# One 12 KB-row transfer per expert item in place of an 8 KB-row and a 4 KB-row transfer, in a two-layer decoder trunk

## What is computed

```
def moe_swiglu(x, router, w_gate, w_up, w_down):
    '''Top-2-of-8 expert SwiGLU; each routed token is processed only by its selected experts.'''
...
    def block_ffn(args):
        tok, gate, e = args
        xb = xt[tok]
        h = jax.nn.silu(xb @ w_gate[e]) * (xb @ w_up[e])
        return (h @ w_down[e]) * gate[:, None].astype(x.dtype)
```

## Time and profile before

| | |
|---|---|
| median of 3 runs | 1851.79 us (1851.65 to 1855.87) |
| profiled execution | 1854.4 us |
| its span, first to last instruction | 1852.6 us |
| TensorE busy | 1713.2 us, 92% |
| VectorE busy | 1385.1 us, 75% |
| ScalarE busy | 959.0 us, 52% |
| 16 DMA engines, mean over the span | 228 GB/s, 422.46 MB in 76495 packets |
| mean granted TensorE clock | 0.958 |

### The profile page before, as it was taken

The page is one execution under the profiler, slowest core; times in us unless marked ns, Lnnn a source line. Parts: engine busy times, 40 slices in busy tenths (PEclk is TensorE's granted clock), DMA queues, the critical chain, the costliest instruction groups (busy, mean ns, idle before and its releaser), DMA issues.

```text
span 1852.6 us, 35481 instructions
## 1 busy us (share of the span) xinstructions
PE 1713.2 (92%) x13898; PEld 1533.0 (83%) x13898; DVE 1385.1 (75%) x1978; ACT 959.0 (52%) x1439; POOL 125.4 (7%) x99
## 2 busy tenths in 40 slices
PE   6998787899968898799999999999999999999996
PEld 5788766899954467699999899899898998999996
DVE  5355423888869942588888888888888887988985
ACT  1413211555520012477676676677676675776773
POOL 0005100000026630000000000000000000000000
PEclk8999998999988889899999999999999999999998
DMA  7220003554440050299899799799799898898990
GB/s 291 90 91 3 4 2 115 184 181 173 147 182 1 0 221 21 93 359 357 308 357 360 272 359 349 273 352 343 278 356 340 296 354 329 292 363 311 347 344 23
DMA packets 76495, 422.46 MB, mean 228 GB/s; under 512 B 8625, under 2 KB 8881, under 8 KB 41537
## 3 DMA queue, kind: packets, MB, share of 16 engines
q1 hardware_dynamic: 75744, 418.18, 60.8%
q0 software_dynamic: 608, 2.15, 0.3%
HBM read 419.24 MB, written 1.05 MB: 227 GB/s over the span
## 4 chain that ended last, share of the span: by engine, by line
PE 83%; DVE 11%; issue 4%; ACT 2%; POOL 0%; DMA 0%; DVEq 0%; POOLq 0%; ACTq 0%; SPq 0%
PE PS L1041 33%; PE PS L1057 16%; PE PS L928 10%; PE PS L594 8%; DVE SA L1405 2%; DVE SGS L1413 2%; PE PS L1065 2%; PE PS L915 2%; DVE WLO L1437 1%; PE PS L1049 1%; PE PS L576 1%; PE PS L740 1%; DVE SA L1398 1%; PE PS L757 1%; PE PS L609 1%
## 5 line engine op out<-in xcount | busy, mean ns | idle before, releaser
L1437 DVE TENSOR_TENSOR WLO<-EXA,WHI 128x1024 fp32r<-128x1024 f32 x448 | 530.2, 1221 | 89.0 <-ACT WHI L498 88.5
L1041 PE MATMUL PS<-WHI,XGH 128*128 128x256 f32 x1792 | 514.6, 287 | 20.3 <-issue 14.1
L1041 PE MATMUL PS<-WLO,XGH 128*128 128x256 f32 x1792 | 511.6, 285 | 0.0
L1041 PE MATMUL PS<-WHI,XGL 128*128 128x256 f32 x1792 | 511.4, 285 | 0.0
L498 ACT ACTIVATE WHI<-EXA 128x1024 fp32r<-128x1024 f32 x448 | 450.3, 1060 | 0.0
L1041 PEld LDWEIGHTS PS<-WHI,XGH 128*128 128x128 f32 x1792 | 344.1, 192 | 31.3 <-issue 16.2
L1041 PEld LDWEIGHTS PS<-WLO,XGH 128*128 128x128 f32 x1792 | 344.3, 192 | 8.0
L1041 PEld LDWEIGHTS PS<-WHI,XGL 128*128 128x128 f32 x1792 | 344.4, 192 | 0.0
L1442 DVE TENSOR_TENSOR WLO<-EXB,WHI 128x1024 fp32r<-128x1024 f32 x224 | 272.8, 1218 | 2.4 <-ACT WHI L504 2.4
L504 ACT ACTIVATE WHI<-EXB 128x1024 fp32r<-128x1024 f32 x224 | 236.2, 1055 | 7.9 <-PE PS L1057 7.9
L523 ACT ACTIVATE MSG<-PS 128x128 f32<-128x128 f32 x224 | 62.2, 277 | 301.0 <-PE PS L1041 295.1
(11 more groups left out here) (357 smaller groups left out, 2602.9 us busy)
## 6 DMA issues: line engine op xcount, KB each, us to landing
EXA<-in_wmoe SPq DMA_DIRECT2D x224, 1024.0 KB, 7.5
EXB<-in_wmoe SPq DMA_DIRECT2D x224, 512.0 KB, 5.5
FRA<-in_wffn SPq DMA_DIRECT2D x22, 1024.0 KB, 5.9
RING<-in_wsq SPq DMA_DIRECT2D x16, 1024.0 KB, 4.9
FRB<-in_wffn SPq DMA_DIRECT2D x22, 512.0 KB, 3.8
GLUW<-in_wglu SPq DMA_DIRECT2D x8, 1024.0 KB, 12.6
LORA<-in_lora SPq DMA_DIRECT2D x1, 1536.0 KB, 22.3
LORA<-in_lora SPq DMA_DIRECT2D x1, 1152.0 KB, 19.1
```

Source lines behind the costliest of these rows:

```text
L1041: mm = pe.matmul(PS[:, n % 2, 0:T], x[:, k, :], w[:, n % 2, cols], start=k == 0 and m == 0, stop=k == KC - 1 and m == 2)
L1437: tt(WLO[:, n % 2, cols], EXA[n % NSLOT][:, cols], WHI[:, n % 2, cols].bitcast(F32), ALU.subtract)\
```

## The change

The two arrays of slots become one array `EX` of seven slots of 12 KB, in the same memory; an item's weights come with one transfer, `load_item`, and one semaphore per slot (`m_in0` and so on). The transfer waits for `m_blo` of item n - 7, which comes after that item's `m_alo`. The first five items go out without a wait; items 5 and 6 wait for `glu_used`, where A of item 5 did not.

```
-        EXA = [at(f"EXA{n}", [P, NARROW], F32, o) for n, o in enumerate((r(0), r(8), r(16), r(24), r(32), 0, 8))]
-        EXB = [at(f"EXB{n}", [P, D], F32, o) for n, o in enumerate((r(40), r(44), r(48), r(52), r(56), 16, 20))]
+        EX = [at(f"EX{n}", [P, WIDE], F32, o) for n, o in enumerate((r(0), r(12), r(24), r(36), r(48), 0, 12))]
...
-        def expert_in(part, b, n):
-            return S(f"m{part}_in{n % NSLOT}"), (b * (FM // NSLOT) + n // NSLOT + 1) * 16
+        def expert_in(b, n):
+            return S(f"m_in{n % NSLOT}"), (b * (FM // NSLOT) + n // NSLOT + 1) * 16
...
-            def load_a(b, n, ex):
-                sp.dma_start(EXA[n % NSLOT][:, :], wmoe[ex * FM + n][:, 0:NARROW]).then_inc(expert_in("a", b, n)[0], 16)
-
-            def load_b(b, n, ex):
-                sp.dma_start(EXB[n % NSLOT][:, :], wmoe[ex * FM + n][:, NARROW:WIDE]).then_inc(expert_in("b", b, n)[0], 16)
+            def load_item(b, n, ex):
+                sp.dma_start(EX[n % NSLOT][:, :], wmoe[ex * FM + n]).then_inc(expert_in(b, n)[0], 16)
...
             for n in range(5):
-                load_a(0, n, 0)
-                load_b(0, n, 0)
-            load_a(0, 5, 0)
+                load_item(0, n, 0)
             sp.wait_ge(S("glu_used"), 2)
-            load_b(0, 5, 0)
-            load_a(0, 6, 0)
-            load_b(0, 6, 0)
+            load_item(0, 5, 0)
+            load_item(0, 6, 0)
             for n in range(NSLOT, FM):
-                sp.wait_ge(S("m_alo"), 2 * (n - NSLOT + 1))
-                load_a(0, n, 0)
                 sp.wait_ge(S("m_blo"), n - NSLOT + 1)
-                load_b(0, n, 0)
+                load_item(0, n, 0)
...
                 for n in range(FM):
-                    sp.wait_ge(S("m_alo"), b * (2 * FM) + 2 * (n - NSLOT + 1))
-                    load_a(b, n, ex)
                     sp.wait_ge(S("m_blo"), b * FM + n - NSLOT + 1)
-                    load_b(b, n, ex)
+                    load_item(b, n, ex)
...
-                act.activation(WHI[:, n % 2, cols], EXA[n % NSLOT][:, cols], ACT.Copy).then_inc(S("m_ahi"), 1)
+                act.activation(WHI[:, n % 2, cols], EX[n % NSLOT][:, cols], ACT.Copy).then_inc(S("m_ahi"), 1)
```

More of the change, by code:

```diff
@@ L495, in hi_a @@
                 if h == 0:
-                    act.wait_ge(*expert_in("a", b, n))
+                    act.wait_ge(*expert_in(b, n))
                 cols = slice(h * D, (h + 1) * D)
-                act.activation(WHI[:, n % 2, cols], EXA[n % NSLOT][:, cols], ACT.Copy).then_inc(S("m_ahi"), 1)
+                act.activation(WHI[:, n % 2, cols], EX[n % NSLOT][:, cols], ACT.Copy).then_inc(S("m_ahi"), 1)
             def hi_b(b, n, down_done=True):
-                act.wait_ge(*expert_in("b", b, n))
+                act.wait_ge(*expert_in(b, n))
                 if down_done:
                     act.wait_ge(S("m_used"), b * FM + max(n - 1, 0))
-                act.activation(WHI[:, n % 2, NARROW:WIDE], EXB[n % NSLOT][:, :], ACT.Copy).then_inc(S("m_bhi"), 1)
+                act.activation(WHI[:, n % 2, NARROW:WIDE], EX[n % NSLOT][:, NARROW:WIDE], ACT.Copy).then_inc(S("m_bhi"), 1)
             hi_a(0, 0, 0)
@@ L1436, in lo_a @@
                 cols = slice(h * D, (h + 1) * D)
-                tt(WLO[:, n % 2, cols], EXA[n % NSLOT][:, cols], WHI[:, n % 2, cols].bitcast(F32), ALU.subtract)\
+                tt(WLO[:, n % 2, cols], EX[n % NSLOT][:, cols], WHI[:, n % 2, cols].bitcast(F32), ALU.subtract)\
                     .then_inc(S("m_alo"), 1)
@@ L1441, in lo_b @@
                 dve.wait_ge(S("m_bhi"), b * FM + n + 1)
-                tt(WLO[:, n % 2, NARROW:WIDE], EXB[n % NSLOT][:, :], WHI[:, n % 2, NARROW:WIDE].bitcast(F32), ALU.subtract)\
+                tt(WLO[:, n % 2, NARROW:WIDE], EX[n % NSLOT][:, NARROW:WIDE], WHI[:, n % 2, NARROW:WIDE].bitcast(F32), ALU.subtract)\
                     .then_inc(S("m_blo"), 1)
```

## The result

The changed kernel takes 1866.1 us in the median of five runs, the kernel before 1851.8 us beside it: 1.0067 of its time, 95% interval 1.004 to 1.0093. It is slower, by 14 us between the medians here. In a later session the changed kernel took 1866.7 us, 1.008 of the kernel before (1.0063 to 1.0097). No change was forecast, with a range up to 1857, so the forecast was wrong, and the page shows at once where it was right and where not.

What follows compares the result with a forecast made beforehand. TensorE was taken to bound the kernel, with loads hidden. Four terms of 0 and +0.8 us at the loop's return took the 1851.8 us median to 1852.6, stated as 1852.5 us; range 1847 to 1857 us.

Steps and rivals of the forecast that it cites:

- Rival A: Weight stream inside the blocks falls below 360 GB/s and sets TensorE's pace: +24 us, 1876 us; chance 4 in 100.
- rival C: Weight stream binds now and the merge relieves it: 1823 us, likelier 1837; chance 8 in 100 together with shorter return stalls.
- the lead: Item loads, issue to ScalarE's read: the 8 KB part starts one item later, tightest lead 16.2 us, cost 0.
- The landing: Time for an item's single 1.573 MB transfer to arrive: 7 us taken, at most 9.8, covered by the lead.
- the step on the loop's return: Starts of loop rounds 2 to 6: instruction packets wait behind longer weight rows, +0.8 us, bounds -3.1 and +5.0.
- Rival B: TensorE's stalls at the loop's return grow and keep the clock low: 1861.9 us; chance 5 in 100 to pass 1857.4.
- the +3.4 us for the clock: Part of the +5.0 bound: lower clock lasting as long at the two better returns as at the three worse, 2 x 1.7.

Runs made afterwards that it cites:

- the small part first: Kernel before, with both parts of an item issued together behind the `m_blo` wait, 4 KB rows before 8 KB rows: 1855.9 us, 1.0015.

## Why the prediction was wrong

**Right: TensorE bounds the blocks, and the loads are hidden.** 4.37 us per item at the full clock and 217 waits for slots. Rival A (too slow a stream) and rival C (the merge relieves the stream) are both refuted: no wait for a load appeared, and the blocks ran no faster.

**Right: the lead.** It fell by an item and cost nothing, as the small part first shows. The landing was mis-sized: 7 us, at most 9.8, were forecast, 8.5 and 10.6 measured. The tightest lead, item 8 issued at 784.96 and read at 801.16 us, is 16.2 us and covers it.

**Wrong: the step on the loop's return.** It was priced at +0.8 us with +5.0 as the bound. It is +9.0 us in the profiles of the first session and +10.0 in those of the second, by the stalls alone. The step took one row of weights for the unit that the fetch waits behind, 0.47 us of 12 KB in place of 0.31, and argued that since the bytes in flight are the same, nothing more could come. It also counted two packets per return, of which one stands between branch and restart. Both arguments were wrong: the row's length has no part in it (rows of 4 KB in one transfer: 27.4 us), and equal bytes are not equal waits, since the order and the size of the transfers decide how many of them stand ahead. The sum by the rows that the packets show: before, eight rows of 4 KB stood ahead of the fetch on its engine, 8 x 0.16 = 1.3 us, now 6.6 of 12 KB in the mean, 6.6 x 0.47 = 3.1 us. The estimate of 1.8 us per return fits the 1.8 and 2.0 us measured in the two pairs of profiles.

The rows for this were there: the two instruction packets stood in the earlier trace rows, the stalls in the earlier trace rows, and B of an item issued just ahead of A of the next, 0.37 us apart, in the earlier trace rows. What was not asked is what SyncE has in flight when TensorE jumps.

The page "DMA: Bandwidth & Descriptors" of the Trainium skill, section "Queues, rings and completion order", was cited for the +0.8 us, and misread. It says that an engine drains a whole packet, typically 9 to 17 descriptors and at most 64, from one queue before it takes another, while what this profile counts as a packet is one row. A transfer over 128 partitions gives each of 16 engines 8 rows and a semaphore write, 9 descriptors. By that rule the fetch waits out the share of the transfer that stands first. The trace agrees where that is 512 or 1024 KB in two-transfer form: 20 returns of 20 in four profiles. It does not agree at 1536 KB, where the packet went one or two rows before the end of eight, and four or five before the end of 24, in 15 returns of 15. There the measurement decides.

**Rival B** named the mechanism and the place, gave it 5 in 100 and 1861.9 us, and set its point of decision at stalls over 3.75 us. Its condition came true: stalls over 4 us with 0.72 at all five returns. It was right in kind and not in its terms: it had 1.6 us for the stalls, by the same unit, where 9.0 came, and 8.5 us for the clock, where the two pairs of profiles show -1.3 and +1.6 us. That 1861.9 us is the nearest of the stated times is luck. The same reading is behind the +3.4 us for the clock in the stated bound: a window's mean was taken for time at half rate, though part of it lies in the stall.

**What is still open.** From the first load to the end the changed kernel took 1192.0 us in both profiles, the kernel before 1183.8 and 1180.6: 9.8 us, of which the stalls are 9.5 and the clock 0.2. The medians differ by 11.5 us (both in one session), 13.2 and 14.3 us. The part before the experts was 2.1 us longer in the mean of two profiles each, well within its own spread. The last 2 to 4 us between the medians are thus not placed. That the packet of 16 KB is TensorE's code is inferred; the trace doesn't name its owner. But in all 60 returns of the twelve profiles TensorE's first matrix multiplication comes 1.5 to 1.8 us after the packet's end, while the packet starts anywhere from 0.9 to 4.6 us after the branch. Why those 1.5 to 1.8 us are needed wasn't tried, nor why the packet passes before the end of a 1536 KB transfer and not before the end of a smaller one.

## What to carry to other kernels

In this kernel a loop's return fetches code through the DMA engines that carry the data, and a load issued just ahead of it makes TensorE wait for all or most of that load. So look at what is in flight at each jump of the bounding engine, and hold that load back by a step, or put a small transfer in front: here one added `+ (n == 5)` was worth about 18 us. When transfers are merged "with the same bytes", ask who else stands in the queue.

## What was not expected of the hardware

- The wait of an instruction packet goes by the size of the transfer first in the queue, not by row length: sums over five returns of 26.3 and 26.8 us for 1536 KB (27.4 with 4 KB rows), 23.6 for 1024 KB, 17.2, 16.8, 17.4 and 18.5 for 512 KB, 13.9 for 256 KB, and 9.9 to 11.1 with nothing in flight. On its engine it passed exactly between two transfers of 512 and 1024 KB, but inside one of 1536 KB, after 72 to 84 KB.
- 12 KB rows landed no sooner than 8 and 4 KB rows: one item as one transfer landed in 8.5 us in the median, as three pieces of 4 KB rows in 8.7, and as an 8 KB-row part in 7.5 us with the 4 KB-row part issued 0.37 us ahead of it.
- Two profiles of one kernel granted 0.86, 0.72, 0.72, 0.86, 0.72 and 0.86, 0.72, 0.86, 1.00, 0.72 of the clock after stalls of 3.0 to 3.75 us, with 24.1 and 17.6 us of TensorE's work at the lower clock: 3 us of cost between two executions of one kernel.
- A longer stall can cost less clock: 3.8 to 5.4 us of work per return at the lower clock behind stalls of 5.0 to 5.6 us, up to 6.1 us behind stalls of 3.2 to 3.8 us, as the slow stretch began 1.4 to 3.0 us before the longer ones ended. Behind stalls of 1.9 to 2.4 us it began up to 1.5 us after the restart, and each time it was 3.4 us.
